# A layer norm's channel means: one averaging matmul over a sum of four tiles, in place of four matmuls

## The reference, cut to what matters

```
def layer_norm(x, g, b):
    mu = jnp.mean(xf, axis=-1, keepdims=True)
    var = jnp.mean(jnp.square(xf - mu), axis=-1, keepdims=True)
    y = (xf - mu) * lax.rsqrt(var + NORM_EPS)
    return (y * g + b)

def conformer_conv_branch(pc, dw_w, dw_b, ln_g, ln_b, w_pw, b_pw):
    c = pc[..., :CONV_CH] * jax.nn.sigmoid(pc[..., CONV_CH:])
    c = causal_depthwise_conv(c, dw_w, dw_b)        # 31 taps
    c = jax.nn.silu(layer_norm(c, ln_g, ln_b))
    return c @ w_pw + b_pw
```

## Time and profile before

| | |
|---|---|
| median of three runs | 2026.19 us |
| span of the profiled execution | 2024.2 us (its own total time is not listed beside it) |
| TensorE matmul, busy | 2001.7 us, 99% |
| VectorE, busy | 1221.0 us, 60% |
| ScalarE, busy | 1025.0 us, 51% |
| GpSimd, busy | 284.7 us, 14% |
| mean granted clock of TensorE | 0.998 of full speed |
| averaging matmuls (line 2244) | 32 records, 379 ns each |

### The profile page before, as it was taken

The page is one execution under the profiler, slowest core; times in us unless marked ns, Lnnn a source line. Parts: engine busy times, 40 slices in busy tenths (PEclk is TensorE's granted clock), DMA queues, the critical chain, the costliest instruction groups (busy, mean ns, idle before and its releaser), DMA issues.

```text
span 2024.2 us, 26360 instructions
## 1 busy us (share of the span) xinstructions
PE 2001.7 (99%) x9813; PEld 1649.0 (81%) x9828; DVE 1221.0 (60%) x1374; ACT 1025.0 (51%) x1318; POOL 284.7 (14%) x365
## 2 busy tenths in 40 slices
PE   8999999999999999999999999999999999999998
PEld 6888888788888888887788888787778888788886
DVE  5555798865555555898855555555555555545554
ACT  5444685744445445586654445544444445455443
POOL 1000469200000000568100002111100000000000
PEclk9999999999999999999999999999999999999999
DMA  7554554445555554554455544344335554415552
GB/s 269 195 186 173 178 199 168 173 178 187 186 187 200 186 186 178 172 211 165 175 179 197 189 173 169 144 146 142 129 125 193 188 188 174 171 65 200 188 189 96
DMA packets 54626, 354.15 MB, mean 175 GB/s; under 512 B 7696, under 2 KB 8336, under 8 KB 12816
## 3 DMA queue, kind: packets, MB, share of 16 engines
q1 hardware_dynamic: 53968, 352.51, 49.1%
q10 hardware_dynamic: 576, 0.53, 0.1%
HBM read 351.97 MB, written 1.05 MB: 174 GB/s over the span
## 4 chain that ended last, share of the span: by engine, by line
PE 91%; DVE 5%; ACT 2%; issue 1%; DVEq 1%; DMA 0%; SPq 0%; POOLq 0%; ACTq 0%; POOL 0%
PE psum L1946 64%; PE psum L1997 18%; DVE wlo L1107 3%; PE psum L2075 2%; PE psum L2012 1%; PE psum L2415 1%; PE psum L2436 1%; PE psum L1958 1%; PE psum L2422 1%; ACT whi L586 1%; PE psum L2123 0%; PE psum L2152 0%; DMA raw<-w_stream 0%; DVE psum L1330 0%; PE psum L2276 0%
## 5 line engine op out<-in xcount | busy, mean ns | idle before, releaser
L1107 DVE TENSOR_TENSOR wlo<-raw,whi 128x2048 fp32r<-128x2048 f32 x325 | 752.0, 2317 | 388.5 <-ACT whi L586 386.0
L1946 PE MATMUL psum<-whi,xTh 128*128 128x512 f32 (+1 forms) x1920 | 764.3, 398 | 2.5 <-DVE xTl L1124 1.8
L1946 PE MATMUL psum<-whi,xTl 128*128 128x512 f32 (+1 forms) x1920 | 745.9, 388 | 0.0
L1946 PE MATMUL psum<-wlo,xTh 128*128 128x512 f32 (+1 forms) x1920 | 745.7, 388 | 0.0
L586 ACT ACTIVATE whi<-raw 128x2048 fp32r<-128x2048 f32 x325 | 622.0, 1916 | 239.8 <-PE psum L1997 151.3
L1946 PEld LDWEIGHTS psum<-whi,xTh 128*128 128x128 f32 x1920 | 361.2, 188 | 79.5 <-issue 7.1
L1946 PEld LDWEIGHTS psum<-whi,xTl 128*128 128x128 f32 x1920 | 361.1, 188 | 76.0
L1946 PEld LDWEIGHTS psum<-wlo,xTh 128*128 128x128 f32 x1920 | 361.7, 188 | 68.1
L1997 PE MATMUL psum<-whi,braT 128*128 128x512 f32 x1056 | 337.8, 390 | 0.0
L1997 PEld LDWEIGHTS psum<-whi,braT 128*128 128x128 f32 x1056 | 198.2, 188 | 41.2
L1997 PE MATMUL psum<-wlo,braT 128*128 128x512 f32 x528 | 205.5, 389 | 0.0
(11 more groups left out here) (260 smaller groups left out, 1467.6 us busy)
## 6 DMA issues: line engine op xcount, KB each, us to landing
raw<-w_stream SPq DMA_DIRECT2D x326, 1024.0 KB, 4.8
bias<-chunks SPq DMA_DIRECT2D x18, 256.0 KB, 5.1
x<-x_in SPq DMA_DIRECT2D x2, 512.0 KB, 5.6
raw<-w_stream SPq DMA_DIRECT2D x4, 256.0 KB, 7.1
arena<-gate_w SPq DMA_DIRECT2D x2, 512.0 KB, 5.2
arena<-fins SPq DMA_DIRECT2D x2, 512.0 KB, 5.5
con<-consts SPq DMA_DIRECT2D x1, 720.0 KB, 10.8
out<-x ACTq DMA_DIRECT2D x2, 256.0 KB, 2.3
```

The lines of the kernel that those rows point to most:

```text
L1107: TT(wlo[:, r], raw[:, r], whi[:, r].bitcast(F32), ALU.subtract).then_inc(lo_done, 1)
L1946: ins = pe.matmul(dst(rb), s(kt)[:, rows], w[:, r, at_:at_ + cols], start=start and n == 0 and k == 0, stop=stop and n == len(kts) - 1 and ...
```

## The change

VectorE first adds the four channel tiles of `cacc` into one tile (two adds, 128x512 and 128x256, with a drain between), in a new region `csum` which lies at the start of the convolution's padded input. It does so behind the last tap and ahead of `largest(3)`, and waits for both engines' taps there. The averaging matmul then runs once on that tile and waits for the sum. The squares are added in place the same way, behind the subtraction of the mean and ahead of `upto(26)`, after a wait for the squares, and their averaging matmul runs once too.

```diff
-        csq = region(o_conv, 4, S)
+        csq, csum = region(o_conv, 4, S), region(o_conv, 2, S)
...
+                def tiles_summed(dst, src, what):
+
+                    TT(dst[:, 0:2], src[:, 0:2], src[:, 2:4], ALU.add)
+                    dve.drain()
+                    TT(dst[:, 0], dst[:, 0], dst[:, 1], ALU.add).then_inc(what, 1)
...
                 conv(TAPS)
+                dve.wait_ge(conv_done, M + 1)
+                dve.wait_ge(conv_pool, M + 1)
+                tiles_summed(csum, cacc, conv_summed)
                 largest(3)
                 upto(25)
                 reciprocals(3)
...
                 TT(cacc, cacc, over(psum[:, 4, 0:S], 4), ALU.subtract).then_inc(cent_done, 1)
+                dve.wait_ge(sq_done, M + 1)
+                tiles_summed(csq, csq, sq_summed)
                 upto(26)
...
-                def channel_mean(src, dst, what):
-
-                    for t in range(4):
-                        ins = pe.matmul(dst, mean_w[:], src[:, t], start=t == 0, stop=t == 3)
-                    ins.then_inc(what, 1)
-
                 def means():
-                    pe.wait_ge(conv_done, M + 1)
-                    pe.wait_ge(conv_pool, M + 1)
-                    channel_mean(cacc, psum[:, 4, 0:S], mean_in)
+                    pe.wait_ge(conv_summed, M + 1)
+                    pe.matmul(psum[:, 4, 0:S], mean_w[:], csum[:, 0], start=True, stop=True).then_inc(mean_in, 1)
...
                 def variances():
-                    pe.wait_ge(sq_done, M + 1)
-                    channel_mean(csq, psum[:, 5, 0:S], var_in)
+                    pe.wait_ge(sq_summed, M + 1)
+                    pe.matmul(psum[:, 5, 0:S], mean_w[:], csq[:, 0], start=True, stop=True).then_inc(var_in, 1)
```

More of the change, by code:

```diff
@@ L355, in program @@
         rope_q, rope_k, conv_pool = sem("rope_q"), sem("rope_k"), sem("conv_pool")
+        conv_summed, sq_summed = sem("conv_tiles_summed"), sem("sq_tiles_summed")
         ix_done, scan_done = sem("i_times_x"), sem("scan_done")
```

## The result

The changed kernel takes 2033.1 us, the median of five runs (2032.92 to 2035.14); the kernel before takes 2026.18 (2026.12 to 2026.45). The ratio is 1.0041 [1.003, 1.0052]: slower by 6.9 us. The profiled span grew from 2024.2 to 2031.3 us, by 7.1.

A forecast was written before the change was run, and what follows sets the result against it. TensorE is 99% busy, but VectorE's chain was taken to set TensorE's restart at 384.71 in the first mixer layer, likewise in the second. Span 2024.2 + 8.5 (2 x 4.23) + 2.0 = 2034.7 us, range 2031.0 to 2038.0.

The forecast's parts named there:

- who gets in between the adds: Channel sum: GpSimd's waiting merge enters at the drain between VectorE's two adds, ends 368.52; second add ends 368.81.
- TensorE's saving: Four averaging blocks lose six of eight passes each, 4.6 to 5.2 us, counted as 0 ahead of TensorE's wait.
- The sum of squares: Adds behind ScalarE's Square, 1.21 us in VectorE's idle time, done half a us before ScalarE's split; price 0.
- The sum of channels: Adds between last taps and maxima, taking turns with GpSimd; slot 27's low part 4.23 us late a layer.
- rival 1: VectorE keeps the turn between its two channel adds; 3.35 late a layer, 6.7 in all, 2032.9; chance 0.14.
- Rivals 1 to 3: First two have their own lines; the third: no exclusion decides, 1.1 us slower in all, 2027.3; chance 0.06.
- Rival 2: Narrow adds don't exclude GpSimd, only slot 27's low part does; 2.64 late a layer, 5.3 in all, 2031.5; chance 0.10.
- Rival 4: The averaging blocks are on the path, so TensorE's saved 4.6 to 5.2 us count: about 2021.2; chance 0.06.
- The first wait: TensorE idle 3.6 to 3.9 us before the averaging matmul at 365 us, until VectorE's channel sum is done.
- The second wait: TensorE waits 1.9 us for the sum of squares, until about 377.7.
- rival 5: TensorE's clock falls after new waits; covered behind the first, else up to 1.7 a layer: 2036.4 or 2038.1; chance 0.14.
- the term 2.0 + the span of before: Profiled span 2024.2 us plus 2.0, by which the timed median of 2026.19 exceeds it, taken to stay.

The follow-up runs named there:

- squares_only: The changed kernel with only the sum of squares on VectorE, the channel mean again four matmuls; 2025.91 us, ratio 1.0000 against the kernel before.
- psum_sum: The changed kernel with the channel sum as three 128x256 adds gathered in PSUM, only the first with two SBUF inputs; 2031.27 us, ratio 1.0027.
- reduce_pool_later: The changed kernel with the channel sum as one reduction and GpSimd's second bias half held until slot 27's low part is written; 2029.97 us, ratio 1.002.
- reduce_once: The changed kernel with the channel sum as one VectorE reduction over four tiles in place of add, drain, add; 2030.55 us, ratio 1.0022.
- after_pool_later: The changed kernel with GpSimd's second half of the bias work held back until slot 27's low part is written; 2027.67 us, ratio 1.0011.

## Why the prediction was right

**Direction, mechanism and size** held: 2034.7 was forecast, 2033.1 came, within the range. One choice on the way, who gets in between the adds, came out right for a reason that the rows do not bear out (below).

- **TensorE's saving is worth nothing.** Right. In `squares_only` the saved matmuls went into TensorE's wait at y11 (1.40 us in place of 0.61, time unchanged). The block of the means was never saved without its sum; with it TensorE waited 3.48 us at that very matmul.
- **The sum of squares is worth nothing.** Right: 0.69 + 0.08 + 0.42 = 1.19 us, forecast 1.21, with 0.61 us to spare before the split, forecast 0.5; as the only change (`squares_only`), ratio 1.0000.
- **The sum of channels costs 4.23 a layer.** It cost 4.13 and 4.14. Its steps, in the run's own time: first add ends 366.41 (forecast 366.25, and the run is 0.18 later throughout), merge 368.61 (368.52), second add 368.89 (368.81), low part 372.15 (372.07). The early start of the maxima and the low part's return to 2.28, which gives 0.78 back, are both there.
- **GpSimd gets in between the adds.** The outcome is right: its merge ran between them, 2.49 us long. The reason given, that the drain between the adds lets it in, isn't shown, and in this the choice was lucky. Both cases of the earlier trace rows are a tensor_scalar of GpSimd (line 1794), and the merge is a tensor_tensor. In the first of them the two engines did not even take whole turns: VectorE's pair at 250.82 took its undisturbed 0.88 us while GpSimd's instruction ran until 251.44. The same trace has cases of the right kind, at `scan(0)`, `scan(1)`, the low part, `scan(2)`, `scan(3)`, where VectorE has no drain at all (kernel before, VectorE, then GpSimd):
```profile
291.07 1.58 DVE L1384 TENSOR_TENSOR_SCAN arena<-arena 128x256 f32<-128x256 f32 x2
292.58 2.49 DVE L1107 TENSOR_TENSOR wlo<-raw,whi 128x2048 fp32r<-128x2048 f32 x1
294.99 1.76 DVE L1384 TENSOR_TENSOR_SCAN arena<-arena 128x256 f32<-128x256 f32 x2
```
```profile
292.07 0.85 POOL L1770 TENSOR_TENSOR arena<-arena,mcos 128x128 f32<-128x128 f32 x1
292.88 2.51 POOL L1771 TENSOR_TENSOR arena<-arena,msin 128x128 f32<-128x128 f32 x1
297.14 0.46 POOL L1775 TENSOR_TENSOR arena<-arena 128x128 f32<-128x128 f32 x1
```
  The second scan ends at 292.65. GpSimd's tensor_tensor, waiting since 292.07, ends at 292.92 (0.46 us is such a one undisturbed), and the low part, dispatched at 292.58, ends 2.15 after that, at 295.07. Then the next of GpSimd's, waiting since 292.88, ends at 295.39, ahead of the scan dispatched at 294.99. Of VectorE's pairs without a drain there are four such cases in each layer, and GpSimd's waiting tensor_tensor went in between in all eight. So these rows speak for the forecast and against rival 1 with or without a drain; why the tensor_scalar at 300.35 was passed over at 302.52 stays open, and no run took the drain away.
- **What excludes what** held. The Trainium skill (SBUF — State Buffer, "Who interferes with whom") says that a VectorE instruction with at most one SBUF input, outside the two-port modes, doesn't contend with GpSimd, one with two SBUF inputs contends with a GpSimd instruction that reads SBUF, and a tensor_reduce never contends on this chip. `psum_sum` (2.15 against 0.43 and 0.42 us) and `reduce_pool_later` (1.97 against 1.99 beside GpSimd) agree.
- **Rivals 1 to 3** fall by the same rows: no add of 0.42 behind a 2.3 one, no short adds while GpSimd ran. Rival 2 (narrow adds don't exclude) would have been the near miss: `psum_sum` and `reduce_once`, built so that the sum isn't stuck between GpSimd's turns, come out at 2.62 and 2.66 late, where rival 2 said 2.64. Rival 4 falls with `squares_only`.
- **The first wait** was forecast at 3.6 to 3.9 us and is 3.48: the forecast counted from the start at which the matmul would have stood, 365.12, and the idle time counts from the end of the one before.
- **The second wait** was forecast at 1.9 us, until 377.7. TensorE did go on at 377.70, but had waited only 0.31. The clock had fallen behind the first wait and used up the rest, the covered case of rival 5. Uncovered falls are no idle thought either: `after_pool_later` has one.
- **The sum's own error** is the term 2.0 + the span of before, not the price of a step: 2 x 4.13 in place of 2 x 4.23 is 0.2 us; 0.3 is added between the layers and 0.2 at the start; -1.6 comes from the low-clock spell at 1478.6 in the profiled run of before, which I carried over as if it were the kernel's own and which the changed kernel's run didn't have; and the time around the span was 1.8, not 2.0. Together 2034.7 - 0.2 + 0.5 - 1.6 - 0.2 = 2033.2; the profiled run took 2033.07.

Open: why the clock falls behind the 2.1-us idle time in one execution and not in another, and where the 0.3 us between the layers is from. Most of it appears between 930 and 940 us, still ahead of the second norm, where GpSimd's taps meet VectorE at other moments: a low part there takes 2.56 us, and 2.28 in before.

## What to carry to other kernels

Before moving work from a busy engine to a less busy one, see which of the two is on the chain of waits at that very place: here an engine busy for 60% set the time while the one at 99% was waiting for it. Then look at what GpSimd does at that moment: a VectorE tensor_tensor with two SBUF inputs waits for the whole of GpSimd's tensor_tensor, and GpSimd's next one, if it is already waiting, goes in between two of VectorE's. So 1.1 us of adds cost 4.8, and splitting work into two instructions costs a second turn. A sum that must stand beside GpSimd is made with one operand in PSUM, or GpSimd's work is put elsewhere, after a look at what it will meet there. Here neither made a gain of the channel sum: the best version with it (`after_pool_later`) is still 1.6 us over the kernel before.

## What the runs showed of the hardware

- A waiting tensor_tensor ends at the other's end plus its own duration less 0.12 to 0.18 us, for instructions from 0.42 to 2.38 us long, on either engine (366.41, 368.61, 368.89 in the changed kernel; 370.88 in `reduce_once`; 370.68 in `psum_sum`).
- GpSimd's tensor_tensor that was already waiting went in between two instructions of VectorE with both inputs in SBUF in all eight cases without a drain in the kernel before (such as 292.92 and 295.39), and between the two adds with one. A tensor_scalar of GpSimd behaved otherwise: it was passed over at 302.52, and ran beside VectorE's pair at 250.82.
- Adds of 128x256 with one of two inputs in PSUM took 0.43 and 0.42 us beside a GpSimd instruction; with both in SBUF 2.15 and 2.40.
- A reduction in SBUF that reads four tiles at a stride, 128x1024 to 128x256, took 1.97 to 1.99 us, more than the two adds with their drain (1.19). I had worked it out too short.
- Behind an idle time of 3.48 us TensorE's granted clock was 0.51 and 0.50, in both layers. Behind the 2.1-us idle time near 1480 us, which all ten kernels have, it was low in four of the ten profiled executions. In `reduce_pool_later` it stayed at 1.00 behind 2.76 us in the first layer and was 0.50 behind 2.74 in the second.
- Executions of one kernel are spread over some 3.5 us (before: 2024.16 to 2027.92), the worth of two such low-clock spells; a difference of 1 us needs many of them.
